# A float32 decoder stack on one core: expert weights in 21 transfers of 2 MB per task in place of 42 of 1 MB

## The reference, cut to what matters

```python
def moe_swiglu(h, w_router, w_gate, w_up, w_down):
    t = h.reshape(b * l, d)
    logits = jnp.matmul(t, w_router).astype(jnp.float32)
    top_val, top_idx = lax.top_k(logits, TOP_K)              # TOP_K = 2 of 8 experts
    gates = jax.nn.softmax(top_val, axis=-1)
    combine = jnp.sum(jax.nn.one_hot(top_idx, N_EXPERTS, dtype=jnp.float32) * gates[..., None], axis=1)
    for e in range(N_EXPERTS):
        y_e = swiglu(t, w_gate[e], w_up[e], w_down[e])       # 1024 x 3584, 1024 x 3584, 3584 x 1024
        out = out + combine[:, e:e + 1] * y_e
```

## Time and profile before

| | |
|---|---|
| median of 3 runs | 2110.19 us (2105.21 to 2112.29) |
| the profiled execution's own time | 2114.78 us |
| its span, first to last instruction | 2113.0 us |
| mean granted TensorE clock | 0.951 of full speed |
| TensorE busy in the span | 1924.5 us (91%) |
| VectorE, ScalarE, GpSimd busy | 1441.1, 1204.5, 253.2 us |
| read from HBM | 493.31 MB |
| expert transfers | 3 x 112 of 1 MB each |

### The profile page before, as it was taken

How to read it: one execution, slowest core, us unless ns; L and a number is a source line. 1 busy time by engine, 2 the same in 40 slices (tenths; PEclk the granted TensorE clock), 3 DMA queues, 4 the chain that set the end, 5 groups by cost and what they waited for, 6 DMA issues and landing times.

```text
span 2113.0 us, 27404 instructions
## 1 busy us (share of the span) xinstructions
PE 1924.5 (91%) x10193; PEld 1655.2 (78%) x10193; DVE 1441.1 (68%) x1293; ACT 1204.5 (57%) x1117; POOL 253.2 (12%) x241
## 2 busy tenths in 40 slices
PE   5996688998799989886869999999999999999997
PEld 4785578997699979875758878787887878888785
DVE  3544655566554448645348888888888888888886
ACT  3445334444343446545337767677767767777775
POOL 1001202000000000013010040310404013040300
PEclk9997899999799989998969999999999999999999
DMA  7532044555255535430059999999999989999894
GB/s 244 187 134 80 0 159 142 196 180 186 69 194 169 172 120 169 151 120 1 10 201 374 355 334 378 319 376 335 350 357 344 370 323 362 344 357 373 317 372 153
DMA packets 215373, 495.22 MB, mean 234 GB/s; under 512 B 10436, under 2 KB 16898, under 8 KB 215314
## 3 DMA queue, kind: packets, MB, share of 16 engines
q1 hardware_dynamic: 212928, 493.06, 66.0%
q0 software_dynamic: 288, 1.05, 0.1%
q10 hardware_dynamic: 2098, 0.28, 0.1%
HBM read 493.31 MB, written 1.05 MB: 234 GB/s over the span
## 4 chain that ended last, share of the span: by engine, by line
PE 85%; DVE 7%; ACT 5%; issue 2%; ACTq 1%; DMA 0%; DVEq 0%; SPq 0%; POOL 0%
PE ps L235 26%; PE ps L237 25%; PE ps L236 25%; PE ps L1969 1%; PE ps L2030 1%; DVE w_lo L230 1%; PE ps L1988 1%; PE ps L319 1%; DVE a_lo L1541 1%; ACT a_hi L1023 1%; PE ps L1916 1%; PE ps L1895 0%; DVE x_res L1274 0%; ACT arena L297 0%; ACT arena L983 0%
## 5 line engine op out<-in xcount | busy, mean ns | idle before, releaser
L230 DVE TENSOR_TENSOR w_lo<-raw,w_hi 128x2048 fp32r<-128x2048 f32 x470 | 1073.1, 2294 | 388.3 <-ACT w_hi L223 388.1
L223 ACT ACTIVATE w_hi<-raw 128x2048 fp32r<-128x2048 f32 x470 | 899.8, 1919 | 442.5 <-PE ps L237 441.4
L235 PE MATMUL ps<-w_hi,a_hi 128*128 128x512 f32 (+3 forms) x1952 | 770.6, 395 | 18.8 <-DVE w_lo L230 11.4
L237 PE MATMUL ps<-w_hi,a_lo 128*128 128x512 f32 (+3 forms) x1952 | 760.1, 389 | 0.0
L236 PE MATMUL ps<-w_lo,a_hi 128*128 128x512 f32 (+3 forms) x1952 | 759.4, 389 | 0.0
L235 PEld LDWEIGHTS ps<-w_hi,a_hi 128*128 128x128 f32 x1952 | 371.5, 190 | 97.4 <-issue 9.9
L237 PEld LDWEIGHTS ps<-w_hi,a_lo 128*128 128x128 f32 x1952 | 370.8, 190 | 76.1
L236 PEld LDWEIGHTS ps<-w_lo,a_hi 128*128 128x128 f32 x1952 | 371.5, 190 | 73.7 <-issue 1.7
L235 PE MATMUL ps<-a_hi,w_hi 128*128 128x256 f32 x960 | 274.0, 285 | 3.3 <-issue 3.0
L236 PE MATMUL ps<-a_lo,w_hi 128*128 128x256 f32 x960 | 273.2, 285 | 0.0
L237 PE MATMUL ps<-a_hi,w_lo 128*128 128x256 f32 x960 | 273.1, 284 | 0.0
(11 more groups left out here) (292 smaller groups left out, 1261.6 us busy)
## 6 DMA issues: line engine op xcount, KB each, us to landing
raw<-in_moe_w_gate_dram SPq DMA_DIRECT2D x112, 1024.0 KB, 6.9
raw<-in_moe_w_up_dram SPq DMA_DIRECT2D x112, 1024.0 KB, 7.1
raw<-in_moe_w_down_dram SPq DMA_DIRECT2D x112, 1024.0 KB, 6.6
raw<-in_ssd_w_in_dram SPq DMA_DIRECT2D x24, 1024.0 KB, 5.2
raw<-in_w_in_dram SPq DMA_DIRECT2D x22, 1024.0 KB, 5.1
raw<-in_w_ffn_in_dram SPq DMA_DIRECT2D x20, 1024.0 KB, 5.1
raw<-in_w_ffn_out_dram SPq DMA_DIRECT2D x11, 1024.0 KB, 5.0
raw<-in_dense_w_down_dram SPq DMA_DIRECT2D x11, 1024.0 KB, 4.9
```

The costliest lines, as they stand in the source:

```text
L223: nc.scalar.activation(w_hi[:, u % SPL, :], raw[:, u % RAW, :], ACT.Copy).then_inc(hi_done, 1)
L230: nc.vector.tensor_tensor(w_lo[:, u % SPL, :], raw[:, u % RAW, :], w_hi[:, u % SPL, :].bitcast(F32), ALU.subtract).then_inc(lo_done, 1)
L235: nc.tensor.matmul(o, lh, rh, start=start, stop=False, skip_group_check=True)
L237: return nc.tensor.matmul(o, ll, rh, start=False, stop=stop, skip_group_check=True)
```

## The change

An expert transfer now brings two units (2 MB) to two neighbouring slots of `raw`, with one step of the semaphore of the first of the two slots, and it waits until the second of the two slots is free. `split_hi` of either unit waits for the semaphore of the pair's first slot. The pairs lie in slots 2 and 3, 4 and 5, 0 and 1. All units outside the expert layer stay as they were.

```diff
@@ -217,7 +217,8 @@
             if u >= LAST:
                 return
-            act.wait_ge(raw_full[u % RAW], 16 * rounds + 16 * (u // RAW + 1))
+            first = u if u < UNIT["moe"] else u - u % 2
+            act.wait_ge(raw_full[first % RAW], 16 * rounds + 16 * (first // RAW + 1))
             if u >= SPL:
                 act.wait_ge(unit_used, RAW * rounds + u - SPL + 1)
             nc.scalar.activation(w_hi[:, u % SPL, :], raw[:, u % RAW, :], ACT.Copy).then_inc(hi_done, 1)
@@ -680,22 +681,20 @@
                 def moe_load(u, src, rounds):
-                    sp.wait_ge(lo_done, RAW * rounds + (M0 + u - RAW + 1))
-                    sp.dma_start(raw[:, (M0 + u) % RAW, :].rearrange("p (k n) -> p k n", k=src.shape[-2]),
-                                 src).then_inc(raw_full[(M0 + u) % RAW], 16)
+                    sp.wait_ge(lo_done, RAW * rounds + (M0 + u + 1 - RAW + 1))
+                    at = (M0 + u) % RAW
+                    dst = raw[:, at:at + 2, :].rearrange("p a c -> p (a c)").rearrange("p (k n) -> p k n", k=src.shape[-2])
+                    sp.dma_start(dst, src).then_inc(raw_full[at], 16)
...
                     def two(u, src, cols, rounds):
-                        for half in range(2):
-                            moe_load(u + half, src[:, bass.ds(e, 1), 4 * half:4 * half + 4, cols]
-                                     .rearrange("p a k n -> p (a k) n"), rounds)
+                        moe_load(u, src[:, bass.ds(e, 1), :, cols].rearrange("p a k n -> p (a k) n"), rounds)
 
                     def down(u, k0, rounds):
-                        for half in range(2):
-                            moe_load(u + half, moe_down_v[:, bass.ds(e, 1), bass.ds(k0 + 2 * half, 2), :]
-                                     .rearrange("p a k n -> p (a k) n"), rounds)
+                        moe_load(u, moe_down_v[:, bass.ds(e, 1), bass.ds(k0, 4), :].rearrange("p a k n -> p (a k) n"),
+                                 rounds)
```

## The result

The changed kernel took 2112.52 us (median of 20 runs, 2110.23 to 2116.58), the kernel before 2109.33 us beside it (20 runs, 2104.09 to 2116.16). The ratio is 1.0018, with a 95% interval from 1.0010 to 1.0027.

A forecast was written before the change was run, and what follows sets the result against it. The prediction took TensorE to bound the expert layer, with DMA hardly less full. It added 2.3 us at the layer's start and 1.0 us for late pairs, 3.3 us, to the median 2110.19, giving 2113.5 us, range 2108 to 2134.

The forecast's parts named there:

- The bound: Expert layer from 1100 us: it goes at TensorE's pace, busy 199.1 of every 200 us, loads having slack.
- signs of being wrong: Expert rounds: ScalarE waiting for `raw`, more than 7 TensorE waits for `w_lo`, rounds over 16.8 us, landings above 10.9 us.
- The margin and the landing: Expert rounds: 8.9 to 10.1 us between a pair's issue and its split, against 7.7 us for a pair alone.
- the 10.9 us beyond which TensorE stops: Expert rounds: TensorE stops when a pair lands later than this after issue; 1.2 us of split lead included.
- the 6.8 that the prediction set beside it: Landing of a pair alone in us, by the skill page's fit: 2.0 us and the bytes over 436 GB/s.
- The lag: Expert rounds: the queue runs behind by 2.8 us at the longest landing; worst case a pair takes 10.5 us.
- the allowance of 1.0 us: Expert layer: cost of late pairs after the 7 changes of task, 1 us in all, between 0 and 7.
- The start: Start of the expert layer: second `split_lo` ends later, delaying TensorE's first gather by 2.3 us (1.9 to 2.7), all showing.
- The sum: Whole kernel: 2.3 us at the layer's start and 1.0 us for late pairs, 3.3 us slower.
- The ring runs dry: Expert rounds: ScalarE waits for pairs, then TensorE for `w_lo`; 17 us slower, up to 66; chance 0.28.
- The start costs nothing: Start of the expert layer: early pair or a gather waiting for something else, no change, 2111 us; chance 0.12.
- Larger transfers free something: Changes of task: TensorE's 6.3 us of idling, were all owed to loads, would go, giving 2107 us; chance 0.04.

The follow-up runs named there:

- e6: Changed kernel with each pair issued two units later still; 1290.3 us from first expert issue to last instruction, against the changed kernel's 1046.9.
- e5: Changed kernel with each pair issued one unit later still; 1110.9 us from first expert issue to last instruction, against the changed kernel's 1046.9.
- e3: Kernel before with both the late issue and the wait for both halves, transfers still 1 MB; ratio to the kernel before 1.0019.
- e11: Repeat of e3, both waits with 1 MB transfers on the kernel before; 1045.5 us from first expert issue to last instruction, as in e3.
- e12: The changed kernel profiled again, nothing edited; 1043.6 us from first expert issue to last instruction, against 1046.9 in its first profile.
- e2: Kernel before with only the wait of a pair's first unit for both halves, 1 MB transfers issued early; ratio to the kernel before 1.0013.
- e4: Changed kernel with each task's first pair loaded as two 1 MB transfers, each unit waiting for its own; ratio to the kernel before 0.9999.
- e8: Changed kernel with VectorE's selection matrix moved ahead of the two first splits; 2105.54 us, ratio 0.9980.
- e7: Kernel before with VectorE's selection matrix (1.3 us) moved ahead of the two first splits; 2100.35 us, ratio 0.9961.
- e1: Kernel before with only the late issue of a pair's first unit, 1 MB transfers, each unit waiting for its own; ratio to the kernel before 1.0004.
- e9: Changed kernel with the down pairs (56 of 168) as two 1 MB transfers; 1046.0 us from first expert issue to last instruction, changed kernel 1046.9.
- e10: Changed kernel with gate and up pairs (112 of 168) as two 1 MB transfers; 1046.4 us from first expert issue to last instruction, changed kernel 1046.9.

## Why the prediction was right

**The bound.** TensorE sets the pace from 1100 us on, and the ring's slack takes what the change does to the loads. That held in the main: 199.1 of 200 us, and TensorE's waits for `w_lo` 6.3 and 6.8 us. It did not hold in full. Of the prediction's own signs of being wrong, ScalarE's waits for `raw` inside the rounds came (32, where it said none but the first), so did a landing above 10.9 us (one, 11.3) and an eighth wait of TensorE for `w_lo`. They cost 1.6 us and not the 17 to 66 of the rival.

**The margin and the landing.** I had 7.7 us for a pair in an empty queue and the 10.9 us beyond which TensorE stops. The first is right within 0.1 us (7.8 in e6, 7.8 at the start of the layer); the 6.8 that the prediction set beside it was 1.0 us short. Behind the first burst 27 of the 168 pairs took over 10 us, the top of the range that I gave. The limit was wrong in its form: it counts the splits' lead of 1.2 us as if each pair had it anew. With one unit less room it would have given 1050 to 1065; e5 took 1110.9, since a late split makes the next issue late, so that the loop decides (landing plus split, 12.0 us for four units' 11.2). In the changed kernel a late pair is followed by pairs in time before long, and the error cost little.

**The lag.** I carried the lag over from the kernel before, 2.8 us at most, and let the size of a transfer do nothing but add bytes. The size does add to it: with both waits alone ScalarE waits 8 us for transfers, with the size 31 to 40 (e3 and e11 against the change and e12). Its price lies in the allowance of 1.0 us with bounds 0 and 7: the four profiles give 0.3 to 2.2, 1.2 on average. The reason I gave for the allowance, late pairs after a change of task, is not the main one: in the first profile the pairs that landed just in time or late lie inside the tasks, above all in the last one.

**The start.** The term of 2.3 us with bounds 1.9 and 2.7 measured 2.1 at the low part. Its reason, the wait for both, is shown by e2 and e4; the 0.2 us less fit the pair's landing at 7.8 rather than 8.05 us. That "all of it shows" left out the clock: at the first scatter it is 2.4 us in e2 and 0.3 in e12.

**The sum.** 3.3 us predicted, 3.2 between the medians, 3.8 by the ratio, and in the stretch 4.0 in the first profile of the changed kernel and 0.7 in the second. That the medians meet the sum within 0.1 us is partly luck: the rounds cost up to 2.2 us for a reason that I did not have, and the start's part depends on the clock's steps. The absolute time, 2113.5, stands beside 2112.52.

**The rivals.** "The ring runs dry" didn't happen, though it was near: one unit less of room costs 64 us (e5). Its ground, a steady rate below 375 GB/s, isn't there: in the changed kernel's first burst the three pairs landed 7.8, 13.3 and 18.7 us after the first issue, so 5.4 us apart, less than the 5.60 that TensorE takes for a pair. "The start costs nothing" falls with e2 and e4. "Larger transfers free something" falls too: the waits at the changes of task are the same 6.3 us and more. The first burst alone was quicker with the size: six units took 18.7 or 18.8 us from the first issue to the last landing (the change, e12, e8), and 19.0 to 19.4 in the kernels with 1 MB there. The Trainium skill, page "DMA: Bandwidth & Descriptors", section "Bandwidth", has the efficiency of a transfer still rising above 1 MB, measured there on transfers that GpSimd issues; the burst agrees in direction. In the rounds the queue already delivers what TensorE takes, and there the pair as one transfer landed later than as two issued together: 8.8 us after the issue in the median, and in e3 8.0 after the first of the two issues.

## What to carry to other kernels

A transfer of two units was as good as two of one only where nothing waited for the first unit by itself and the slack covered the latest landings, not only the usual one. Look at the first use after a pause, where the landing stands on the path, and keep that one small. In a ring of k slots judge a new rule of issue by the loop (issue, landing, every step to the one that frees the slot) against the time the bound engine takes for the same units, not by the lead that one unit happens to have. And where a change costs 2 us at a start, ask what else waits in the same program order: moving 1.3 us of VectorE's work ahead of the two splits (e7) won 8 us, more than any shape of the transfers tried here.

## What the runs showed of the hardware that I had not expected

The last of the 16 steps of a semaphore lags behind the bulk of them. Taken from the steps in the trace, 1100 to 2080 us, the ninth of a pair's 16 comes 7.5 us after its issue in the changed kernel (7.4 to 7.7 in 8 of 10), while the sixteenth comes 1.1 us behind it in the median and 2.7 or more in the worst tenth. With the pair as two transfers of 1 MB, issued as late (e3), it is 0.4 and 1.8. The size is not the only thing that makes it: in the kernel before, with 1 MB and each load issued as early as its slot allows, it is 1.1 and 2.0. In e6, with its nearly empty queue, it is 0.3 and 0.5, with 2 MB. So the long lags came with a full queue, and the longest with 2 MB in it. A unit can be split only when the last step is there. The Trainium skill, page "DMA: Bandwidth & Descriptors", section "Why a DMA increments its semaphore by 16 and not by 1", says that the engines finish independently and only the full count means that all is there; by that rule the slowest engine sets the landing, and the trace agrees.

TensorE's last step from 1.2 to 2.4 GHz at the start came 29.0 us after the first expert issue in the kernel before, e1 and e4, where the first unit doesn't wait for the second. It came at 31.6 to 32.1 us in seven profiles with the wait for both (the change, e2, e3, e11, e9, e10, e5). In e12, the changed kernel again, and in e6 it came at 29.0 (in e6 the clock fell once more, from 46.0 to 49.5 us). Between the two profiles of the changed kernel the first scatter moved by 2.1 us with it.
